# Eight experts of a two-block transformer: from split fp32r products on 128 slots to plain fp32 products in four 32-column strips on 96 slots

## The reference, cut to what matters

```python
logits = h @ router                                # 256 tokens, 8 experts
top_v, top_i = lax.top_k(logits, 2)                # two experts a token
gates = softmax(top_v)
# per expert e, on the rows h[tokens routed to e]:
y_e = (silu(x @ w1[e]) * (x @ w3[e])) @ w2[e]      # 1024 -> 3584 -> 1024
x = x + g2 * sum over the two choices of gate * y_e
out = rms_norm(x, final_g)
```

## Time and profile before

| | |
|---|---|
| median, lowest, highest of three runs | 2097.79, 2093.74, 2098.26 us |
| the profiled execution, first to last instruction | 2095.7 us |
| PE busy | 2013.4 us (96%), 10805 matmuls, 10805 weight loads |
| DVE, ACT busy | 1548.4 us (74%), 1230.5 us (59%) |
| DMA | 545.76 MB, mean 260 GB/s |
| first matmul of the pass loop, last of it | 1111.1 us, 2072 us |

### The profile page before, as it was taken

One profiled execution on the slowest core, in us unless ns is written; L12 is line 12 of the kernel. 1 busy time (PEld: TensorE's weight loads), 2 busy tenths in 40 slices (PEclk: granted clock), 3 DMA queues, 4 the chain that ended last, 5 costly groups with the idle time before them and its releaser, 6 DMA issues.

```text
span 2095.7 us, 28133 instructions
## 1 busy us (share of the span) xinstructions
PE 2013.4 (96%) x10805; PEld 1604.7 (77%) x10805; DVE 1548.4 (74%) x1845; ACT 1230.5 (59%) x1399; POOL 47.8 (2%) x42
## 2 busy tenths in 40 slices
PE   6999998999899989999999999999999999999995
PEld 4785577866688457888877888888888888888884
DVE  4862756856744566665577898898989898888986
ACT  3233544454431555554357777777777777777774
POOL 1000000000000000000000000000000000000000
PEclk8999999999999999999999999999999999999997
DMA  9202522255732856457697999999999999999992
GB/s 329 95 26 97 200 81 70 99 192 190 260 121 81 311 182 230 161 197 179 206 373 263 378 370 380 369 384 378 377 374 372 379 368 386 367 383 374 372 373 90
DMA packets 262813, 545.76 MB, mean 260 GB/s; under 512 B 6410, under 2 KB 41889, under 8 KB 262604
## 3 DMA queue, kind: packets, MB, share of 16 engines
q1 hardware_dynamic: 258352, 530.71, 70.0%
q0 software_dynamic: 3616, 11.69, 1.5%
q10 hardware_dynamic: 764, 2.24, 0.3%
HBM read 538.32 MB, written 6.30 MB: 260 GB/s over the span
## 4 chain that ended last, share of the span: by engine, by line
PE 89%; DVE 5%; DMA 3%; ACT 2%; issue 1%; SPq 0%; POOL 0%; ACTq 0%; POOLq 0%; DVEq 0%
PE bank L782 83%; PE bank L820 2%; PE bank L1449 1%; DMA ring<-in_w_mod 1%; DVE ring_r L2130 1%; DMA ring<-in_attn_w_qkv 1%; PE bank L891 1%; DVE nmax L2167 1%; DMA ring<-in_ada_w 1%; PE bank L852 1%; ACT ring_r L1607 1%; PE bank L1095 0%; DVE H L2050 0%; DVE H_r L2059 0%; DVE H L2079 0%
## 5 line engine op out<-in xcount | busy, mean ns | idle before, releaser
L782 PE MATMUL bank<-H_r,scratch_r 128*128 128x512 f32 x1664 | 573.4, 397 | 1.7 <-DVE H_r L2070 1.4
L782 PE MATMUL bank<-scratch_r 128*128 128x512 f32 x1472 | 422.9, 391 | 0.0
L782 PEld LDWEIGHTS bank<-H_r,scratch_r 128*128 128x128 f32 x1664 | 312.3, 188 | 70.8 <-DVE H_r L2070 3.2
L782 PEld LDWEIGHTS bank<-scratch_r 128*128 128x128 f32 x1472 | 276.9, 188 | 60.0
L2577 DVE TENSOR_TENSOR ring_r<-ring,H_r 128x2048 fp32r<-128x2048 f32 x128 | 293.1, 2290 | 33.1 <-ACT H_r L1902 31.3
L1902 ACT ACTIVATE H_r<-ring 128x2048 fp32r<-128x2048 f32 x128 | 245.9, 1921 | 102.6 <-PE bank L782 102.6
L782 PE MATMUL bank<-H_r,ring_r 128*128 128x256 f32 (+2 forms) x1296 | 302.1, 315 | 1.3 <-ACT H_r L1518 1.3
L782 PE MATMUL bank<-scratch_r,ring_r 128*128 128x256 f32 (+2 forms) x1280 | 277.7, 343 | 7.1 <-ACT ring_r L1607 2.6
L782 PE MATMUL bank<-H_r,modrow_r 128*128 128x512 f32 x672 | 263.2, 392 | 0.0
L782 PE MATMUL bank<-ring_r,scratch_r 128*128 128x512 f32 x896 | 248.1, 391 | 0.0
L2577 DVE TENSOR_TENSOR scratch_r<-scratch,H_r 128x2048 fp32r<-128x2048 f32 x97 | 222.0, 2289 | 34.7 <-ACT H_r L1902 33.5
(11 more groups left out here) (258 smaller groups left out, 2271.3 us busy)
## 6 DMA issues: line engine op xcount, KB each, us to landing
ring<-in_moe_w SPq DMA_DIRECT2D x96, 2048.0 KB, 9.1
scratch<-in_moe_w SPq DMA_DIRECT2D x73, 2048.0 KB, 9.3
ring<-in_ada_w SPq DMA_DIRECT2D x24, 2048.0 KB, 9.2
ring<-in_ff_w SPq DMA_DIRECT2D x14, 2048.0 KB, 7.7
ring<-in_w_mod SPq DMA_DIRECT2D x12, 2048.0 KB, 11.4
ring<-in_ff_w SPq DMA_DIRECT2D x8, 1792.0 KB, 8.2
ring<-in_w_in SPq DMA_DIRECT2D x6, 2048.0 KB, 8.3
ring<-in_attn_w_qkv SPq DMA_DIRECT2D x6, 2048.0 KB, 8.1
```

The costliest lines, as they stand in the source:

```text
L782: m = nc.tensor.matmul(out_, w, x_, start=first, stop=last)
```

## The change

- A pass takes 96 tokens of an expert (`SLOTS`), in three groups of 32. An expert with more takes further passes, up to five in all; the rank and list code handles two thresholds. The list stays at 8 passes where no expert has more than 96 rows.
- Weights, tokens and hidden rows are no longer split. The products are plain fp32.
- `tiles` issues four matmuls with 32 stationary columns each, into the four 32-partition strips of one bank. Strips 0 to 2 hold the three token groups and take one column set of the weights; strip 3 holds group r and takes another set, the fourth, so that after r = 0, 1, 2 the fourth set is done for all groups. In w1 and w3 the columns come in two sets, 0 to 2047 (four times 512) and 2048 to 3583 (four times 384); in w2 the output is four times 256.
- A pass has 24 chunks in 8 slots: w1 and w3 by rows (256 rows of 2048 or 1536 columns, runs of 8 KB or 6 KB), w2 by 512 or 384 rows (runs of 4 KB). The new slot is given free later than the others, at norm 6.
- silu, multiplication and turning now go by bank and set: per pass ACT has 6 silus, 6 copies of turned rows, 2 copies of tokens and 3 copies of result quarters, DVE 6 multiplications and 3 result scalings, PE 21 transposes of hidden rows and 8 of tokens. Rows 96 to 127 of the turned hidden set hold strip 3's part, and `down` reads them with the right group.
- The choice of slots for the next pass is one product of 3 columns (`select`) where there were six.
- SP's extra load after the loop is gone.

The core of the diff:

```diff
-SLOTS = 128
-OVER = 3
+SLOTS = 96
+GROUPS = SLOTS // 32
+OVER = 5
-MOE_RING = 7
+MOE_RING = 8
+LATE_SLOT = MOE_RING - 1
...
+        WIDE = (512, 384)
         def moe_order():
+            up = [[(w, st, q) for q in range(4)] for st in range(2) for w in ("w1", "w3")]
+            down = [[("w2", st, q) for q in range(4)] for st in range(2)]
+            return up[0] + up[1] + up[2] + down[0][:2] + up[3] + down[0][2:] + down[1]
...
-            with pe.Fori(0, passes) as j:
-                halves = iter(half_chunks())
-                def half_products(kind_, i_, parts, last, by_bank=False):
...
+                def tiles(dst, own, other, w, column, last_column, first, last):
+                    for g in range(GROUPS):
+                        product(dst[32 * g:32 * g + 32, :], own(g), w[:, column:column + dst.shape[-1]], first, last)
+                    return product(dst[P - 32:P, :], other, w[:, last_column:last_column + dst.shape[-1]], first, last)
+
+                def up(b0, kind, st, taken, ready, before=lambda r: None, after=lambda q: None):
+                    n = WIDE[st]
+                    for q in range(4):
+                        s, w = moe_chunk(kind, st, q)
+                        for r in range(GROUPS):
+                            if q == 0:
+                                before(r)
+                                pe.wait_ge(taken, j * 6 + (3 * st + r + 1))
+                            for kl in range(2):
+                                k = 2 * q + kl
+                                m = tiles(bank[b0 + r][:, 0:n], lambda g: HE[:, k, 32 * g:32 * g + 32],
+                                          HE[:, k, 32 * r:32 * r + 32], w[:, kl, :], n * r, n * GROUPS, k == 0, k == KT - 1)
...
+                def down(st, q):
+                    s, w = moe_chunk("w2", st, q)
+                    rows = (4, 3)[st]
...
+                    for i in range(rows):
...
+                        for r in range(GROUPS):
+                            dst = bank[6 + r // 2][:, LAT * (r % 2):LAT * (r % 2) + LAT]
+                            m = tiles(dst, part, part(r), w[:, i, :], LAT * r, LAT * GROUPS, first and r != 1,
+                                      last and r != 0)
+                    m.then_inc(weights_used[s], 1)
+
+                pe.wait_ge(tokens_taken, j * 2 + 2)
+                up(0, "w1", 0, silu_done, silu_bank)
...
+                select(5)
+                up(3, "w3", 0, turned_taken, mult_bank, ...)
+                up(0, "w1", 1, silu_done, silu_bank, after=lambda q: turn_hidden(0) if q == 1 else None)
+                pe.wait_ge(down_taken, j * 3 + 3)
+                down(0, 0)
+                down(0, 1)
+                up(3, "w3", 1, turned_taken, mult_bank)
+                down(0, 2)
+                turn_hidden(1)
+                down(0, 3)
+                turn_tokens()
+                for q in range(4):
+                    down(1, q)
```

More of the change, by code:

```diff
@@ L220, in build @@
         landed_at.append(total[slots[i]])
-    moe_slots = list(range(RING, MOE_RING)) + sorted(used_last, key=used_last.get)
+    moe_slots = list(range(RING, LATE_SLOT)) + sorted(used_last, key=used_last.get) + [LATE_SLOT]
     with ExitStack() as ctx:
@@ L613, in build, with pass_done @@
         SPLIT_BEFORE = SPLIT1 + len(FF_HALVES)
[L614 to L653, removed]
+        assert len(moe_order()) == 3 * MOE_RING
+        LAST_SLOT = moe_slots[(len(moe_order()) - 1) % MOE_RING]
         used_base = loads + [1] * (MOE_RING - RING)
         landed_base = total + [0] * (MOE_RING - RING)
+        def pass_done(j):
+            return weights_used[LAST_SLOT], j * 3 + (used_base[LAST_SLOT] + 3)
         OUT = view(0, 2, D)
@@ L1327, in _ @@
             upper = tab[:, T_UPPER:T_UPPER + P]
[L1328 to L1330 removed]
+            group([(upper, MASK[:, 0, 0:EXPERTS])], lambda bk: bk[:, 0:EXPERTS])
+            group([(ones, MASK[:, 0, 0:EXPERTS]), (upper, MASK[:, 1, 0:EXPERTS])], lambda bk: bk[:, 0:EXPERTS])
+            group([(MASK[:, tt, :], tab[:, T_ONES:T_ONES + 1]) for tt in range(2)],
+                  lambda bk: bk[0:2 * EXPERTS, 0:1])
             counted = t.g - 1
@@ L1337, in gather_half, with select @@
                         f = P * (4 * half + k)
-                        last = product(bank[5 + half][:, P * k:P * k + P], H2T[:, tt, f:f + P],
-                                       PICK[:, 0, tt, :], tt == 0, tt == 1)
-                last.then_inc(pass_ready[5 + half], 1)
+                        last = product(bank[5 + half][:, SLOTS * k:SLOTS * k + SLOTS], H2T[:, tt, f:f + P],
+                                       PICK[:, tt, :], tt == 0, tt == 1)
+                last.then_inc(tokens_ready, 1)
+            def select(b):
+                for tt in range(2):
+                    last = product(bank[b][0:SLOTS, 0:3], PICK[:, tt, :], OF_SLOT[:, tt, :], tt == 0, tt == 1)
+                last.then_inc(select_ready, 1)
             assert not release
@@ L1395, in gates @@
-            def gates():
-                for c, of in enumerate(((1, lambda tt: tab[:, T_ONES:T_ONES + 1]),
-                                        (0, lambda tt: RESULT_COL[:, tt:tt + 1]))):
-                    for tt in range(2):
-                        last = nc.tensor.matmul(bank[7][:, c:c + 1], PICK[:, of[0], tt, :], of[1](tt),
-                                                start=tt == 0, stop=tt == 1)
-                        if release:
-                            last.then_inc(release.pop(0), 1)
-                last.then_inc(pass_ready[7], 1)
@@ L1884, in _ @@
             b, n = t.next()
-            take(ACT.Copy, HIDDEN[:, 0:LAT], bank[b][:, 0:LAT], b, n)
+            take(ACT.Copy, ROUTED[:, 0:LAT], bank[b][:, 0:LAT], b, n)
             t.skip(2)
@@ L2457, in _ @@
             x = residual(2, 5, LAT, x, 5, before=down_lows)
-            for s in range(RING, MOE_RING):
+            for s in range(RING, LATE_SLOT):
                 dve.sem_inc(weights_used[s], 1)
```

438 lines of the change are left out of this document (191 added, 247 removed).

## The result

| | before | after |
|---|---|---|
| median of 6 runs each | 2097.97 us | 2105.05 us |
| lowest to highest | 2092.9 to 2099.32 | 2103.16 to 2108.3 |
| profiled execution, span | 2095.7 us | 2103.2 us |
| mean granted clock of TensorE | 0.980 | 0.965 |

The ratio of after to before is 1.0042, 95% interval 1.0028 to 1.0055: slower by 0.4%, where 1.6% faster was forecast. 2105 lies outside the range of 2041 to 2094.

What follows compares the result with a forecast made beforehand. PE was taken as the bound, busy 120.0 of 120.0 us a pass. Span 2095.7 - 55.2 (products) + 21.0 (jumps back) + 0.9 (loop's end) = 2062.4; with 2.1 for the median 2064.5, rounded 2065 us; range 2041 to 2094.

Steps and rivals of the forecast that it cites:

- The price of the products: PE's work in the pass loop: 113.1 us a pass against 120.0, 55.2 us less over 8 passes.
- The number of ACT's operations: ACT in a pass: 14 operations of at most 0.75 us besides small ones, gaining nothing by itself.
- The jump back: PE's branch to the pass loop's start: waits 3.0 us for code not kept, 7 times, 21 us.
- rival 2: At the loop's branch back: the stall also drops the clock, 23 us more, 2088; chance 0.13.
- Rival 1: At the loop's branch back: code is kept or its fetch hidden, no stall, 2044; chance 0.22.
- Rival 3: In w2: PE cannot be fed instructions fast enough, 4.9 us a pass longer, 2104; chance 0.11.
- Rival 4: In the pass loop: DMA rate falls below 371 GB/s; at 350, 2120; chance 0.04.
- the DMA floor: Loads of a pass: 44.8 MB at 386 GB/s take 116.1 us, above PE's 113.1, but stay hidden.
- Refetching: Code of the pass loop: body of 11.5 blocks; if not kept, each pass fetches 11 or 12 again.

Runs made afterwards that it cites:

- 1,330 instructions: The kernel before, with an increment of an unused semaphore behind every third product of a pass: 2097.08 us, ratio 1.0006.
- 1,660 instructions: The kernel before, with one increment of an unused semaphore behind each product of a pass: 2150.6 us, ratio 1.0263.
- light loads: The changed kernel, loop kept, each weight load from the second pass on bringing only its first row of blocks: 2076.5 us, ratio 0.9912.
- the hint at the head: The changed kernel, loop kept, with a hint naming the jump back at the head of the loop body: 2084.35 us, ratio 0.9951.

## Why the prediction was wrong

- **The price of the products** (113.1 us a pass, 55.2 us gained): right. 113.0 us measured, and 57 us between the two kernels without jumps. The widths pay in proportion: a pass's w2 is 27.8 us for 504 of its 672 records, 0.055 a record, 0.22 a group of four, where 0.215 was taken. In one unbroken run of them it is 15.68 us for 288 records, 0.218 a group, with the end of the last record in it. The 512-column groups are at most 21.0 / 48 = 0.44 and the 384-column ones 23.8 / 72 = 0.33, where 0.43 and 0.32 were taken. The number of ACT's operations was wrong (14, where the list of the change gives 17), and nothing rested on it.
- **The jump back: the step that failed.** It stood as "I take 3.0, as a fetch is a load too, behind full queues: 7 back edges, 21 us". Measured are 9.1 us a jump, 63.5 us. It was mis-sized in three parts. The idle time was bounded by 2.7 us, the time of a small load from issue to landing; the gap is 5.0 to 5.3 us beside full queues, and still 3.1 to 3.4 where their share in the gap is 0.85. A second gap of 0.7 to 1.3 us in four of the seven passes had no term. And the restart at a granted clock of 0.50, 2.4 to 3.9 us a pass, was left to rival 2, held less likely since the stretch of the earlier trace rows was sparse before its idle: here PE was full ahead of the gaps, and the clock fell behind all seven.
- **Rival 2** named the right mechanism and still gave 2088, since it stood on the same 3.0 us. Its row had 6.7 us at a granted clock of 0.50 after an idle of 2.07 us, so 3.3 us a pass and the 23 us of its sum; the passes lose 2.4 to 3.9 behind 5.2 us. With the measured loss (9.0 a pass, idle and slow) the forecast's own sum gives 2095.7 - 55.2 + 63 + 0.9 = 2104.4, and 2103.2 was the span.
- **Rival 1** (2044) is what the list is worth without a stall: 2037, 7 us less than its figure. Of these, 2.4 lie in the seven passes from scaling to scaling (841.0 - 790.3 = 50.7 us, where 7 x 6.9 = 48.3 was taken), the rest ahead of them and in the spread of the runs. It was not what happened, since the code is not kept, but it is reached by writing the passes out.
- **Rival 3** (feeding of instructions in w2) did not come: 0.22 us a group in 504 records without a gap.
- **Rival 4 and the DMA floor**: not reached, but the rate was wrong. 386 GB/s was no limit; 400 was held over whole passes with runs of 6 and 8 KB.
- **Refetching** was foreseen (11 or 12 blocks a pass; 13 or 14 came), by the length of the body against 5 blocks seen kept. That a jump to code that is not kept costs time is borne out: 0 us a jump at 1,330 instructions (56 blocks in all), 7.6 at 1,660 (121 blocks). How much is kept beyond 5 blocks, which no row told, lies between the two: 5.2 blocks are kept, 6.5 are fetched anew.

## What to carry to other kernels

Ahead of counting what a new list saves, count its instructions: a loop body beyond what the sequencer keeps (here between 1,330 and 1,660 instructions) paid at every jump, 6 to 10 us beside full DMA queues. Where trips are few, write them out and keep the loop for the rare rest. Price a stall with the clock that it costs, and under the load that will stand beside it.

## What the runs showed of the hardware

- A TensorE loop of some 1,330 instructions is kept whole (56 blocks in all, as with 1,160); one of 1,660 is fetched anew in every iteration, nine blocks for 6.5 blocks of code. Why more blocks come than the code fills is not shown.
- A jump cost 6.1 to 7.6 us in the kernel before (0.22 us a product, PE idle for 3.4 to 4.3 us at it) and 9.1 to 9.7 us with strips (idle for 5.0 to 5.9 us), from scaling to scaling. Why the idle time differs is not shown.
- Straight code of 12 blocks a pass, fetched all along beside 400 GB/s of weights, cost PE nothing: 113.00 busy of 113.00.
- All ten idle times of 5.0 to 5.9 us at a jump (the changed kernel, and with two passes in the body) were followed by a granted clock of 0.50 to 0.53 in the first 1.5 us; two longer stretches, of 3.4 and 3.8 us, are at 0.50 throughout. All ten of 3.4 to 4.3 us in the kernel before had the fall too: 0.50 to 0.53 in the first 1.5 us with 1,660 instructions, 0.50 to 0.64 with two passes in the body. Shorter ones were not always: with light loads five of seven gaps of 3.1 to 3.4 us (0.50 to 0.77 in the first 1.5 us), with the hint at the head six of seven of 2.5 to 2.8 us (0.50). Behind the seventh (1225.8 to 1228.5) the clock stayed at 1.00:

```profile
1228.60:1234.00 5.40, 5.40 (x52) 1.65 (x56) 0.21 (x2) 0.00 (x0) 0.00 (x0) 1.00 1.00 404
```

- Four strips of 32 columns in plain fp32 held four records of 512 columns in 0.43 to 0.44 us, of 384 in 0.33 and of 256 in 0.22 over a whole pass (192 records in 21.0 us, 288 in 23.8, 504 in 27.8).
